# The windowed attention of a two-block model on one Trainium2 core: one more step between scores and exponentials

## The reference, cut to what matters

```
def gqa_attend(q, k, v, bias=None, sink=None):
    s = jnp.einsum("bqhgd,bkhd->bhgqk", q, k) * ATTN_SCALE
    if bias is not None: s = s + bias
    if sink is not None: p = softmax(concat([s, sink_col]))[..., :-1]
    return jnp.einsum("bhgqk,bkhd->bqhgd", p, v)
...
def b_block(args):          # for each of the 8 blocks of 128 queries
    blk, qb = args          # keys: 256 of context, and 384 around the block,
    ...                     # masked to |key - query| <= 128
    return gqa_attend(qb, kk, vv, bias, sink)
...
y_lat = concat([oa * silu(ag), ob * silu(bg)]) @ w_out
oa_c, ob_c = attention of the 256 context queries over the context keys alone
```

## Time and profile before

| what | value |
|---|---|
| time, median of 3 runs | 3090.73 us (3089.06 to 3091.13) |
| time of the profiled execution | 3088.21 us |
| its span in the trace | 3086.4 us |
| PE busy over the span | 2965.4 us, 96% |
| DVE busy over the span | 1528.4 us, 50% |
| attention B, first fill to the output products after it | 672.94 to 867.14 us |

### The profile page before, as it was taken

The page is one execution under the profiler, slowest core; times in us unless marked ns, Lnnn a source line. Parts: engine busy times, 40 slices in busy tenths (PEclk is TensorE's granted clock), DMA queues, the critical chain, the costliest instruction groups (busy, mean ns, idle before and its releaser), DMA issues.

```text
span 3086.4 us, 27627 instructions
## 1 busy us (share of the span) xinstructions
PE 2965.4 (96%) x11230; PEld 1514.8 (49%) x11230; DVE 1528.4 (50%) x1901; ACT 766.0 (25%) x937; POOL 658.0 (21%) x426
## 2 busy tenths in 40 slices
PE   7998999998899999999999999999999999999998
PEld 4564445644455444445764455454444444444443
DVE  4645996327856676744773521145444333344003
ACT  3114772124400201114641123022012222220001
POOL 0002874003500222235441100001111222212110
PEclk9999999998899899999999899999999999999999
DMA  6011000110042211123231011100211111103111
GB/s 224 27 35 41 1 1 28 55 43 1 1 171 102 96 41 41 41 56 92 49 101 48 15 34 35 35 28 21 86 50 41 41 55 41 41 28 119 47 39 55
DMA packets 43374, 162.41 MB, mean 53 GB/s; under 512 B 5520, under 2 KB 6032, under 8 KB 40048
## 3 DMA queue, kind: packets, MB, share of 16 engines
q1 hardware_dynamic: 37008, 143.18, 13.6%
q0 software_dynamic: 6240, 17.47, 2.3%
HBM read 148.04 MB, written 15.20 MB: 53 GB/s over the span
## 4 chain that ended last, share of the span: by engine, by line
PE 88%; DVE 8%; ACT 2%; issue 1%; DMA 1%; POOL 0%; SPq 0%; DVEq 0%; ACTq 0%
PE ps L903 33%; PE ps L896 15%; PE ps L1634 9%; PE ps L1516 4%; PE ps L1473 2%; PE ps L1359 2%; PE ps L1214 2%; PE ps L1179 2%; PE ps L1091 2%; PE ps L1106 2%; PE ps L1120 2%; PE ps L999 1%; PE ps L1025 1%; DVE arena L2341 1%; PE ps L1504 1%
## 5 line engine op out<-in xcount | busy, mean ns | idle before, releaser
L896 PE MATMUL ps<-arena 128*128 128x512 f32 x1280 | 476.5, 533 | 13.1 <-ACT arena L1735 10.9
L903 PE MATMUL ps<-arena 128*128 128x512 f32 x1096 | 481.2, 593 | 3.2 <-DVE arena L2543 1.6
L896 PEld LDWEIGHTS ps<-arena 128*128 128x128 f32 x1280 | 243.8, 192 | 240.7 <-issue 230.4
L903 PEld LDWEIGHTS ps<-arena 128*128 128x128 f32 x1096 | 207.7, 190 | 265.2 <-issue 261.0
L903 PE MATMUL ps<-x_lat,arena 128*128 128x512 f32 x688 | 303.9, 592 | 0.0
L903 PEld LDWEIGHTS ps<-x_lat,arena 128*128 128x128 f32 x688 | 130.7, 190 | 164.5 <-issue 164.5
L1634 PE MATMUL ps<-arena 128*128 128x512 f32 x416 | 179.8, 592 | 0.0
L2518 DVE SCALAR_TENSOR_TENSOR x_ctx<-arena,vectors,x_ctx 128x1024 f32<-128x1024 f32 x120 | 169.6, 1413 | 3.5
L1179 PE MATMUL ps<-arena 64*128 64x512 f32 x504 | 151.5, 682 | 20.6 <-DVE x_ctx L2341 7.7
L1718 ACT ACTIVATE arena<-x_lat 128x1024 f32<-128x1024 f32 x40 | 41.8, 1049 | 436.0 <-PE ps L1634 224.9
L903 PE MATMUL ps<-x_lat,x_ctx 128*128 128x512 f32 x336 | 147.6, 592 | 0.0
(11 more groups left out here) (315 smaller groups left out, 4265.8 us busy)
## 6 DMA issues: line engine op xcount, KB each, us to landing
arena<-in_wall SPq DMA_DIRECT2D x188, 512.0 KB, 3.9
x_lat<-in_xl_in SPq DMA_DIRECT2D x8, 1024.0 KB, 9.9
residual_store<-x_lat SPq DMA_DIRECT2D x8, 1024.0 KB, 6.3
x_lat<-residual_store SPq DMA_DIRECT2D x8, 1024.0 KB, 6.8
x_lat<-expanded_bias POOLq DMA_DIRECT2D x48, 160.0 KB, 3.6
arena<-in_wdown SPq DMA_DIRECT2D x12, 512.0 KB, 4.4
arena<-expanded_bias POOLq DMA_DIRECT2D x32, 160.0 KB, 4.0
out<-x_lat SPq DMA_DIRECT2D x8, 512.0 KB, 3.0
```

Of the source, the lines that this page charges most:

```text
L896: mm = pe.matmul(ps[:, o + c:o + c + n], W[:, ring_of(g) % WSLOTS, k, :], rhs(k, c, n), start=(k == 0), stop=(k == KT - 1))
L903: mm = pe.matmul(ps[:, bank * BANK:(bank + 1) * BANK], weights[:, k, :], tokens[:, k, :], start=(start and k == 0), stop=(k == 3), skip_gr ...
```

## The change

`group_plan` gets a second argument, the distance from the last fill of a group to its first B. Attention A keeps 3, attention B gets 4. NB and B, and PV, OE, DEN, RC, MIX and OM, whose steps are counted from B, all come one step later against F, M and R.

```
-def group_plan(sizes):
+def group_plan(sizes, behind):
...
-        at = max(at + 1, first[g + 1] + 3)
+        at = max(at + 1, first[g + 1] + behind)
...
-            items, first, plan = group_plan([len(gr["keys"]) for gr in groups])
+            items, first, plan = group_plan([len(gr["keys"]) for gr in groups], 3 if name == "A" else 4)
```

## The result

The changed kernel takes 3117.44 us (median of 4 runs, 3112.12 to 3119.19) against 3090.93 (4 runs): ratio 1.0084, 95% interval 1.007 to 1.0098. It is slower by 26.5 us. I had forecast slower, by 13.7, and a range to 3115: the way is right, the size is half of what came, and the range missed it. The profiled execution took 3117.55 us, with a span of 3115.8 against 3086.4.

A forecast was written before the change was run, and what follows sets the result against it. In attention B PE and DVE wait for each other. Interval terms -1 - 1.5 + 3.1 + 2.1 + 7.2 + 2.8 + 1 gave +13.7 us on 3088.2, plus 2.5 for the median: 3104, range 3091 to 3115.

The forecast's parts named there:

- What bounds the stage: In attention B PE and DVE wait for each other, PE partly at half clock; elsewhere PE sets the pace.
- Step 1: DVE's L2374 at each repeat's start waits 1.7 us for POOL's sum, where it waited 2.0 before.
- Step 2: PE's fill of t4 waits 3.9 us for t2's maximum, against 1.34; then half clock until NB ends at 13.9.
- Four repeats "behind the same wait": The clock was low in four successive repeats behind one wait, so all repeats were taken as hit.
- Step 3: DVE's subtraction of t4 and maxima of t3 and t4 finish by 11.5, before NB, so cost nothing.
- Step 4: MIX between M0 and M1 waits for R0, and OM for MIX: 1.2 us idle DVE, 1.5 idle PE.
- Entry and end: Ahead of g3 -1 us (bounds -3 and +1); after g9 +1 us (bounds 0 and +3).
- Rival D: Half clock lasts into fill and product behind NB (+1.9, five times), again after MIX's wait: up to +25, 3116; chance 0.10.
- A: The clock stays full behind PE's wait, saving 13.5 us in all: sum 0, 3091; chance 0.10.
- B: L2374 is free of POOL's sum, so five intervals lose 1.7 us each: +5, 3096; chance 0.08.
- C: POOL's sum misses L2374, PE's wait is 2.2 us and the clock stays full: -8, 3082; chance 0.07.
- The rule of the Trainium skill: A free-running counter judges PE's clock gate, so some repeats could escape half clock; sum between rival A and the forecast.

The follow-up runs named there:

- e3: Changed kernel with POOL's sum of t2 also waiting until DVE has done the next group's two sink operations (L2374, L2375): 3092.22 us, ratio 1.0002.
- e5: Changed kernel with RC, MIX and OM of g3 to g9 one step earlier, where they stood before the change: 3108.92 us, ratio 1.0057.
- e6: Changed kernel with POOL's sum of t2 held behind the sink operations and DEN one step earlier: 3085.61 us, ratio 0.9984.
- e7: Changed kernel with POOL's sum of t2 held behind the sink operations, and DEN, RC, MIX and OM one step earlier: 3074.22 us, ratio 0.9944.

## Why the prediction was right and wrong

- *What bounds the stage* was right: PE and DVE wait for each other, and elsewhere PE sets the pace; what follows the stage shifted whole.
- *Step 1, POOL against L2374*: 1.7 us forecast, 1.78 measured; e3 shows that POOL is the cause.
- *Step 2, the wait*: 3.9 forecast, 3.94 measured, ended by the maximum of t2, and the fill at 2.08. This part held to the tenth.
- *Step 2, what stands behind the wait*: here the prediction failed. I had DEN at 1.87 whatever the clock, and it took 3.43 to the next instruction: 1.5 us per repeat. No DEN in the trace of the kernel before runs inside half clock (all 20 take 1.84 to 2.06), so this price stood in no row, and I took it for nothing where I should have doubled it as I did NB's. And I took the clock as full from NB's end on, while the fill and most of the product behind it ran at half: from the fill behind NB to M0 it is 4.46 us where I had 3.15. Together 2.8 of the 2.9 us by which a repeat of 27.06 exceeds the forecast 24.15. The row for it was at hand: the fill behind the DEN at 717.78 was at 2.08, and I used it for NB alone. Three repeats, from g5 to g8, have this miss, 8.7 of the 14.6 us by which the sum was short.
- *Four repeats "behind the same wait"*, by which I held that all would be hit, was a wrong reading. In the kernel before, NB waits 1.34 or 1.35 us at 764.42, 785.08 and 805.66; at 825.05 it waits 0.21 us, takes 1.78, and the product behind it 1.97. And at 832.88 MIX waits 1.48 us and stays at full clock (1.09). So the length of the wait did not decide it there either.
- *Step 3*, DVE hidden under PE: right. It waited 2.97 us for NB; the copy of t4 stood behind the product of t2, and cost nothing.
- *Step 4, MIX between M0 and M1*: 1.5 and 1.2 us forecast, 1.49 and 1.28 measured. Moving it early gave 8.5 us in all (e5), though not by these two waits in each repeat.
- *Entry and end* were mis-sized: -1 forecast and +2.35 measured, +1 and +3.85, together 6.2 us. At the end M0, M1 and two value products ran at half clock, behind a wait of 1.23 us for a subtraction (ahead of NB, at 852.30) and one of 1.72 for RC; before the same M0 took 0.63:

```profile
856.09 1.98 PE L1214 MATMUL ps<-x_lat,arena 128*64 128x256 f32 x8
...
859.04 1.98 PE L1214 MATMUL ps<-arena 128*64 128x256 f32 x8
```

With M0 at 1.09 us and M1 at 1.12 (0.66 at full), these four alone are 2.7 us. At the entry the fill at 706.67 waited 3.39 us for a maximum, and half clock followed as well.

- *Rival D, the half clock lasts longer*, came in its first half: the fill and most of the product behind NB were hit, 1.3 us and not 1.9, and in three repeats and not five. Its second half did not come: MIX, behind its wait, took 1.09 us and the fill after it 1.13, at full clock. The slower DEN stood in no rival. So it is in part luck that D's upper end, 25 us, lies near the 26.5 measured. I had given it 0.10, though the fill behind the DEN at 717.78 spoke for it. With its +1.9 for each of five repeats the forecast would have been 3113.5.
- *Rivals A, B and C* had the parts right and the sum wrong. B priced the stall at 1.7 per repeat. In e3 its removal was worth 25 us in all, since with the wait at 2.33 in place of 3.94 us the clock stayed full in two of three repeats. C had this mechanism, with a wait of 2.2 us, and I held that 2.67 us spoke against it; at 2.33 us it went both ways.
- *The rule of the Trainium skill* ("TensorE: Matmul & The Clock Gate", "What's actually happening") on the free-running counter, which I set aside: in the changed kernel every wait of 2.44 to 4.12 us ahead of the fill of t4 was followed by half clock. At e3's 2.33 us two repeats escaped and the third was hit, which agrees with the rule; so does e6 at 0.45 us.

## What to carry to other kernels

In a stage where two engines hand work to and fro, don't price a wait by its length: price every instruction of PE behind it at half clock too, thin ones included, until the rows show the full length again. A step that shifts a whole group of operations by one moves some of them into a worse place than the one it was meant for; shift only what the reason asks for, and look at what stands between the wait and the instruction that the other engine needs. A tiny operation of DVE that reads two tensors of SBUF is a place to look at when POOL adds nearby: holding one of its additions back, by some 0.7 us, was worth 10 us in the kernel before, and by 1.1 us it was worth 25 in the changed one.

## What the runs showed of the hardware that I had not expected

- DEN, 16 records of 128x2 products, takes 1.95 us at full clock and 3.58 inside a stretch of half clock. At 717.78 before the change it took 2.06 with a half-clock fill behind it, so it was on the edge of such a stretch and not in it.
- A wait of 2.33 us behind a value product left the clock at full in one repeat and brought it down in the next (e3). Shorter waits went both ways too. Half clock followed 1.34 us behind DEN, and 0.45 us behind DEN at 782.98 in e6. Full clock followed 1.34 us behind M0 (changed kernel, the fill at 739.82), 1.49 us behind a value product (its MIX at 814.87), and 0.45 us behind DEN (e7, at 796.42). So the length of the wait alone does not tell what follows. What does is not shown by these rows, and no run was made to isolate it.
- L2374 waits to the end of a POOL sum that started ahead of it, while the large DVE operations, with one input in PSUM, kept their 1.22 us beside such sums (changed kernel, 797.89 and 799.02, beside POOL's from 797.95 on). The Trainium skill ("SBUF — State Buffer", "Who interferes with whom") has this as an exclusive lock that the later one waits out, for DVE instructions with two SBUF inputs; L2374's fall from 1.78 to 0.17 us in e3 agrees.
